# Hybrid encoder layer on one core: half-loads and a split norm at the start, joined head pairs, and another schedule for the dot products of the first expert stage

## The reference, cut to what matters

```python
h = rms_norm(x, norm1_g); z = h @ w_in            # pool (512) | q (8x64) | k, v (2x64 each)
mix = concat([pool_mixer(zp), gqa_attention(zq, zk, zv)])
x = x + mix @ w_out
xn = rms_norm(x, norm2_g)
q = (xn @ wq).reshape(.., 8, 2, 128); s = einsum(q, subkeys)
sv, si = top_k(s, 16); comb = sv[0] + sv[1]; cv, ci = top_k(comb, 16)
e = i1 * 128 + i2                                   # 16384 experts, 16 for each head and token
g = softmax(cv); a = gelu(einsum(xn, u[e])) * g
out = x + einsum(a, v[e])
```

## Time and profile before

| | |
|---|---|
| device time, median of 3 runs | 1999.72 us (1999.72 to 2002.63) |
| the profiled execution's own time | 1996.21 us |
| its span, first to last instruction | 1994.4 us |
| granted TensorE clock, mean | 0.995 |
| PE busy | 1950.4 us, 98% of the span |
| DVE, ACT, POOL busy | 1640.2, 980.4, 789.3 us |

### The profile page before, as it was taken

The page is one execution under the profiler, slowest core; times in us unless marked ns, Lnnn a source line. Parts: engine busy times, 40 slices in busy tenths (PEclk is TensorE's granted clock), DMA queues, the critical chain, the costliest instruction groups (busy, mean ns, idle before and its releaser), DMA issues.

```text
span 1994.4 us, 28888 instructions
## 1 busy us (share of the span) xinstructions
PE 1950.4 (98%) x10186; PEld 1663.6 (83%) x10186; DVE 1640.2 (82%) x3141; ACT 980.4 (49%) x2048; POOL 789.3 (40%) x588
## 2 busy tenths in 40 slices
PE   7999999999999999999999999799999999999999
PEld 7977998997888888888888888688888888888887
DVE  3866436779999999999987777699998899988997
ACT  5265333333778787777787873222223222223221
POOL 0324110001334333333355555555554555545552
PEclk9999999999999999999999999999999999999999
DMA  6110312125799989988999999899999999999996
GB/s 264 42 35 1 137 53 106 67 98 178 257 319 311 324 299 317 323 283 303 310 359 373 389 380 415 315 388 400 392 405 399 406 395 403 399 390 406 385 404 226
DMA packets 203078, 581.27 MB, mean 291 GB/s; under 512 B 19904, under 2 KB 57152, under 8 KB 200640
## 3 DMA queue, kind: packets, MB, share of 16 engines
q0 software_dynamic: 73728, 268.47, 36.7%
q1 hardware_dynamic: 77616, 243.97, 32.2%
q10 hardware_dynamic: 51600, 67.12, 9.3%
HBM read 505.03 MB, written 74.45 MB: 291 GB/s over the span
## 4 chain that ended last, share of the span: by engine, by line
PE 66%; DVE 4%; DMA 2%; ACT 2%; issue 1%; ACTq 0%; POOL 0%; SPq 0%; DVEq 0%
PE ps L332 20%; PE ps L333 20%; PE ps L334 20%; PE ps L1471 5%; DMA g_dram<-arena_a 1%; DMA arena_a<-in_uT 1%; ACT arena_a L679 1%; DMA ring_b<-in_u_rows,expert_ids 0%; ACT arena_a L683 0%; DVE w_lo L1059 0%; DVE ring_b L1149 0%; ACT arena_b L725 0%; DVE ring_a L1149 0%; DVE y_final L1245 0%; DVE ring_c L1149 0%
## 5 line engine op out<-in xcount | busy, mean ns | idle before, releaser
L332 PE MATMUL ps<-v_hi_slots,w_lo 128*128 128x512 f32 x1024 | 399.1, 390 | 6.2 <-DVE w_lo L1187 6.2
L334 PE MATMUL ps<-v_hi_slots,w_lo 128*128 128x512 f32 x1024 | 399.0, 390 | 0.0
L332 PE MATMUL ps<-feat_hi,w_hi 128*128 128x512 f32 (+1 forms) x936 | 360.0, 385 | 2.0 <-DVE feat_lo L969 2.0
L333 PE MATMUL ps<-feat_lo,w_hi 128*128 128x512 f32 (+1 forms) x936 | 351.2, 375 | 0.0
L334 PE MATMUL ps<-feat_hi,w_lo 128*128 128x512 f32 (+1 forms) x936 | 351.0, 375 | 0.0
L706 ACT ACTIVATE w_lo<-arena_a 128x512 fp32r<-128x512 f32 x128 | 80.9, 632 | 501.7 <-PE ps L334 471.3
L812 POOL DMA_INDIRECT ring_a<-in_u_rows,expert_ids x86 | 114.6, 1333 | 330.9 <-DVE ring_a L1149 169.6
L332 PEld LDWEIGHTS ps<-v_hi_slots,w_lo 128*128 128x128 f32 x1024 | 192.7, 188 | 47.0 <-issue 3.6
L334 PEld LDWEIGHTS ps<-v_hi_slots,w_lo 128*128 128x128 f32 x1024 | 192.7, 188 | 40.0
L334 PEld LDWEIGHTS ps<-feat_hi,w_lo 128*128 128x128 f32 x936 | 176.2, 188 | 31.9
L332 PEld LDWEIGHTS ps<-feat_hi,w_hi 128*128 128x128 f32 x936 | 176.6, 189 | 30.8 <-DVE feat_lo L969 2.2
(11 more groups left out here) (215 smaller groups left out, 4472.7 us busy)
## 6 DMA issues: line engine op xcount, KB each, us to landing
arena_a<-in_v SPq DMA_DIRECT2D x128, 512.0 KB, 9.4
w_raw<-in_uT SPq DMA_DIRECT2D x85, 512.0 KB, 6.6
g_dram<-arena_a ACTq DMA_DIRECT2D x64, 512.0 KB, 9.0
gel_dram<-arena_b ACTq DMA_DIRECT2D x120, 256.0 KB, 5.1
w_raw<-gel_dram SPq DMA_DIRECT2D x120, 256.0 KB, 7.8
arena_a<-in_uT SPq DMA_DIRECT2D x43, 512.0 KB, 6.6
w_raw<-in_w_all SPq DMA_DIRECT2D x17, 1024.0 KB, 5.7
arena_b<-g_dram SPq DMA_DIRECT2D x32, 512.0 KB, 10.9
```

The lines of the kernel that those rows point to most:

```text
L332: nc.tensor.matmul(out, lh, rh, start=first, stop=False)
L333: nc.tensor.matmul(out, lh, rl, start=False, stop=False)
L334: return nc.tensor.matmul(out, ll, rh, start=False, stop=last)
```

## The change

- The first weight block is loaded and split in two halves; xT slice 0 and the small vectors are issued by ACT instead of SP; SP issues the first half, xT slice 1, the second half, then the rest as before.
- PE does nine matmuls on zeroed memory before its first wait for weights; ACT's squares wait for them, since they write the same PSUM area.
- ACT squares x tiles 0 to 2, DVE squares tiles 3 to 5 ahead of `w_split_lo(1)`.
- PE takes `windows(0)` before `flip_qk(0)`; ACT takes `pooled_out(0)` before `flip_out(0)`.
- The scores and the first row maximum of the next head pair are issued within the pair before; DVE's loop over pairs is unrolled.
- The product with w_out takes its k slices in the order 4 to 7, 0 to 3, and waits for the last pair's low parts only ahead of k = 3.
- First expert stage: no dot products up to slab 16, then 2.25 a slab to the end (before: 5/3 a slab from slab 3, 13/5 from slab 81; 249 in all in both). Gate groups spread over 105 slabs for 107, top-k parts over 80 for 82, parameters of tile 0 flipped in slab 5 for 4. With the gate groups `v_first` goes from 113 to 111; SP's wait for the gate stores stays at step 120.
- Second stage: items start one step later, `a_split(1)` is made within the first stage, gate chunk 1 is loaded in steps 0 to 3 instead of ahead of them, `gelu_hid(0)` moves from step 2 to 4.

```diff
 def group_slab(g):
-    return 8 + g * 107 // NG_DEN
+    return 8 + g * 105 // NG_DEN
 def topk_slab(q):
-    return q * 82 // PARTS
+    return q * 80 // PARTS
 def dots_by(e):
-    return 5 * max(min(e - 3, 78), 0) // 3 + 13 * max(e - 81, 0) // 5
+    return 9 * max(e - 16, 0) // 4
 def items_by(e):
-    return min(ITEMS, dots_by(NK - 1) + (ITEMS - dots_by(NK - 1)) * (e + 1) // 126)
+    return min(ITEMS, dots_by(NK - 1) + (ITEMS - dots_by(NK - 1)) * max(e - 1, 0) // 124)
...
-        flip_slab = {t: softmax_step[t] + 3 if t else 4 for t in range(DT)}
+        flip_slab = {t: softmax_step[t] + 3 if t else 5 for t in range(DT)}
...
 @block.sync
-            sp.dma_start(vecs[:, :], io["vecs"]).then_inc(vec_in, 16)
-            load_w(0, 0)
-            for k in range(KD):
+            sp.dma_start(Wr[:, 0, 0:4, :], io["w_all"][0, :, 0:4, :]).then_inc(w_half, 16)
+            load_xt(1)
+            sp.dma_start(Wr[:, 0, 4:8, :], io["w_all"][0, :, 4:8, :]).then_inc(w_in[0], 16)
+            for k in range(2, KD):
                 load_xt(k)
...
-                if e == v_first + 7:
+                if e == v_first + 9:
                     sp.wait_ge(g_out[1], 16 * 4 * (NBLK // 2))
...
-            for piece in range(4):
-                load_gates(1, piece)
...
-                if e >= CH and e % CH < 4 and e // CH + 1 < NK // CH:
+                if e % CH < 4 and e // CH + 1 < NK // CH:
                     load_gates(e // CH + 1, e % CH)
...
 @block.scalar
-            w_split_hi(0)
+            act.dma_start(xst[:, 0, :], io["xT"][:, 0, :]).then_inc(xt_in[0], 16)
+            act.dma_start(vecs[:, :], io["vecs"]).then_inc(vec_in, 16)
+            act.wait_ge(w_half, 16)
+            nc.scalar.activation(Wh[:, 0, 0:4, :], Wr[:, 0, 0:4, :], ACT.Copy).then_inc(w_half_hi, 1)
...
             w_split_hi(1)
-            for t in range(TT):
+            act.wait_ge(warm, 1)
+            for t in range(3):
...
+            pooled_out(0)
             flip_out(0)
-            pooled_out(0)
...
                 if e == 126:
                     a_split_hi(0)
+                    a_split_hi(1)
...
-                if e == 2:
+                if e == 4:
                     gelu_hid(0)
...
 @block.vector
+            for t in range(3, TT):
+                dve.wait_ge(x_in[t], 16)
+                if t > 3:
+                    dve.wait_ge(sq1_dve, t - 3)
+                nc.vector.scalar_tensor_tensor(B_[:, 1536:2560], y[:, t, :], 1.0, y[:, t, :], ALU.mult, ALU.mult,
+                                               accum_out=ss1[:, t:t + 1]).then_inc(sq1_dve, 1)
             w_split_lo(1)
-            dve.wait_ge(sq1, TT)
+            dve.wait_ge(sq1, 3)
+            dve.wait_ge(sq1_dve, 3)
...
             def pair(j, first=False):
-                row_max(j, 0)
+                if first:
+                    row_max(j, 0)
                 for u in range(NU):
                     if u + 1 < NU:
                         row_max(j, u + 1)
+                    elif j < 3:
+                        row_max(j + 1, 0)
...
                 while n < dots_by(e):
-                    if n == dots_by(NK - 3) + 1:
-                        a_split_lo(0)
+                    if dots_by(NK - 3) < n <= dots_by(NK - 3) + 2:
+                        a_split_lo(n - dots_by(NK - 3) - 1)
                     dot(n)
...
+                if n == items_by(e) and e < 4:
+                    v_split_lo(e + 3)
+                    weigh(e + 2)
...
 @block.tensor
-            pe.wait_ge(w_lo, 1)
+            pe.wait_ge(zero_v, 2)
+            for i in range(9):
+                last = mm(ps[:, 7, :], KV_[:, 2 * TOK:2 * TOK + P], KV_[:, 2 * TOK:2 * TOK + 512], start=True, stop=True)
+            last.then_inc(warm, 1)
+            pe.wait_ge(w_half_lo, 1)
             for k in range(KD):
+                if k == 4:
+                    pe.wait_ge(w_lo, 1)
...
             pe.wait_ge(small_in, 16 * len(smalls))
+            pe.wait_ge(z_ev, 6 + 30)
+            windows(0)
             pe.wait_ge(rope_ok, TT // 2)
             pe.wait_ge(rope_dve, TT // 2)
             flip_qk(0)
-            pe.wait_ge(z_ev, 6 + 30)
-            windows(0)
...
                 for u in range(NU):
                     if u + 3 < NU:
                         scores(j, u + 3)
+                    elif j < 3:
+                        scores(j + 1, u + 3 - NU)
...
-            pe.wait_ge(o_lo, 2 + 8)
+            pe.wait_ge(o_lo, 2 + 6)
...
-                    for k in range(KD):
+                    for k in (4, 5, 6, 7, 0, 1, 2, 3):
+                        if k == 3:
+                            pe.wait_ge(o_lo, 2 + 8)
```

More of the change, by code:

```diff
@@ L238, in build @@
         yf = view(yf_, 0, DT, D)
-        small_in = sem("small_in")
+        small_in, warm = sem("small_in"), sem("warm")
+        sq1_dve = sem("sq1_dve")
+        w_half, w_half_hi, w_half_lo = sem("w_half"), sem("w_half_hi"), sem("w_half_lo")
         xt_in = [sem(f"xt_in{i}") for i in range(KD)]
@@ L486, in w_split_hi @@
                 nc.scalar.activation(Wh[:, n % 2, :, :], Wr[:, n % 2, :, :], ACT.Copy).then_inc(w_hi, 1)
-            w_split_hi(0)
+            act.dma_start(xst[:, 0, :], io["xT"][:, 0, :]).then_inc(xt_in[0], 16)
+            act.dma_start(vecs[:, :], io["vecs"]).then_inc(vec_in, 16)
+            act.wait_ge(w_half, 16)
+            nc.scalar.activation(Wh[:, 0, 0:4, :], Wr[:, 0, 0:4, :], ACT.Copy).then_inc(w_half_hi, 1)
             act.wait_ge(vec_in, 16)
             for k in range(KD):
+                if k == 2:
+                    act.wait_ge(w_in[0], 16)
+                    nc.scalar.activation(Wh[:, 0, 4:8, :], Wr[:, 0, 4:8, :], ACT.Copy).then_inc(w_hi, 1)
                 act.wait_ge(xt_in[k], 16)
@@ L754, in _ @@
                     act.wait_ge(a_mm, e)
-                if e + 1 < NK:
+                if 1 <= e < NK - 1:
                     a_split_hi(e + 1)
@@ L847, in newton @@
                 return tt(r, r, tmp[1], ALU.mult)
-            w_split_lo(0)
+            dve.wait_ge(w_half_hi, 1)
+            tt(Wl[:, 0, 0:4, :], Wr[:, 0, 0:4, :], Wh[:, 0, 0:4, :].bitcast(F32), ALU.subtract).then_inc(w_half_lo, 1)
             for k in range(KD):
+                if k == 2:
+                    dve.wait_ge(w_hi, 1)
+                    tt(Wl[:, 0, 4:8, :], Wr[:, 0, 4:8, :], Wh[:, 0, 4:8, :].bitcast(F32), ALU.subtract
+                       ).then_inc(w_lo, 1)
                 dve.wait_ge(ft_hi, k + 1)
@@ L955, in _ @@
             pair(0, True)
-            with dve.Fori(1, 4) as j:
+            for j in range(1, 4):
                 pair(j)
@@ L1359, in pair @@
             def pair(j, first=False):
[L1360 to L1363, removed]
                 if first:
+                    for u in range(3):
+                        if u == 2:
+                            pe.wait_ge(mix_lo, 6)
+                        scores(j, u)
                     windows(3)
@@ L1413, in _ @@
                             Wh[:, ds((c + 1) % 2, 1), k, :].squeeze(1), Wl[:, ds((c + 1) % 2, 1), k, :].squeeze(1),
-                            k == 0, k == KD - 1)
+                            k == 4, k == 3)
                     last.then_inc(y_mm, 1)
```

## The result

The changed kernel takes 2011.01 us (median; 2007.2 to 2012.39), the kernel before 1999.72 (1999.45 to 2005.95): a ratio of 1.0045, with a 95% interval of 1.0027 to 1.0062. It is slower, by 11.3 us from median to median and 8.9 from mean to mean (2001.49 to 2010.43), for 7.8 forecast; the interval is 5.4 to 12.4 us and holds the forecast.

A forecast was written before the change was run, and what follows sets the result against it. PE bounds the kernel, busy 98% of the span, with DVE nearly a bound in the first expert stage. Gains of 27.2 us and losses of 35 make 7.8 slower: 1999.72 to 2007.5 us, range 1995 to 2021 for 8 in 10.

The forecast's parts named there:

- slabs 17 to 80: First expert stage: DVE's list exceeds what PE offers by 34.9 us; 34 lost in all, ends 20 and 42.
- 5.8 of reserve: First expert stage: slack from the end of one slab to the table two slabs on hides 5.8 us of DVE's shortfall.
- The 5 us at the softmax of step 80: End of the long stretch: ACT waits for DVE, 5.8 us later, then loads two tables; 5 us more lost.
- What it said of this stage in the traces: Slabs 17 to 80: 450 to 455 us, DVE over 97% busy, PE waits in most of slabs 30 to 82, DVE's gone.
- Joined pairs: Attention, three seams between head pairs: idle time and half clock behind each go, 7.3 us gained, ends 4 and 8.5.
- The turn: Turn to the second expert stage: gate stores earlier, fewer gathered rows a slab; 16.2 us gained, ends 8 and 16.2.
- Rival B: Turn to second stage: queues stay full, PE again idles for slab 126, 16.2 us not gained, 2023.7 us; chance 0.10.
- The start: Blocks 0 and 1 of z: block 0 begins earlier, block 1 waits for the norm; 1 us lost, 0.4 gained to 2 lost.
- Slab 5 and slab 12: Early first stage: softmax wait and one-hots wait go, about 0.2 us stays; 1.0 us gained, ends 0.5 and 3.5.
- A (the overrun hides): First expert stage: DVE keeps up after all, the 34 us loss falls away, 1973.5 us; chance 0.10.
- C (the pairs don't join): Attention: ACT's loop over pairs stays a loop, so 7.3 us less gain, 2014.8 us; chance 0.06.

The follow-up runs named there:

- e1: Changed kernel with the old pace of dot products (5/3 a slab from slab 3, 13/5 from slab 81): 1984.27 us, ratio to before 0.9922.
- e2: Changed kernel with each dot product over 512 of its 1024 columns, gathers unchanged (leaves out half of each sum): 1975.7 us.
- e12: Changed kernel with 2 dot products a slab from slab 16 for 2.25, the rest left to the second stage: 2015.56 us.
- e7: Changed kernel with DVE's one-hots ahead of the low-part split in every step: 2011.62 us.
- e9: Kernel before with the joined head pairs alone, DVE's loop unrolled: 1994.28 us, ratio 0.9966.
- e4: Kernel before with gate groups over 105 slabs, top-k parts over 80, SP's wait for gate stores kept at step 120: 1996.11 us, ratio 0.9978.
- e3: Kernel before with the new pace of dot products alone (2.25 a slab from slab 16): 2018.89 us, ratio 1.0099.
- e6: Changed kernel with old dot-product pace, norm's mean and root before the split, gate groups over 103 slabs, parts over 79, SP's wait at step 120: 1990.92 us.
- e11: Changed kernel with old dot-product pace to slab 81, then 9/4 a slab, and w_split_lo(1) ahead of DVE's squares: 1987.03 us, ratio to before 0.992.
- e5: Changed kernel with the second weight block's low part made after the norm's mean and root instead of before them: 2010.31 us.
- e10: Changed kernel with the old dot-product pace and w_split_lo(1) ahead of DVE's three squares: 1981.75 us, ratio to before 0.9899.
- e8: Changed kernel without the nine matmuls on zeroed memory and ACT's wait for them: 2012.81 us.

## Why the prediction was right, and which of its terms were not

**The sum and its main cause held.** The step "slabs 17 to 80" foresaw 29 us from DVE's list (457.8 us, against 422.9 that PE offers and 5.8 of reserve); 28.5 were measured. e1 and e2 show the cause from two sides (undo the rule, or halve DVE's time at the same gathers: 422 us both times), e12 its slope, and e7 shows that it isn't an order within the step.

Of the 28.5, 19.0 are idle time of PE and 9.5 stand in the busy column (429.13 for 419.68). e1 runs the same 2168 instructions of PE without the long list, and subtracting the spacings one by one tells what the 9.5 are. The one table more that the change has in the stretch is 0.4 (e1 has 420.10). Two stretches of 3.4 us at half clock, from 597.0 and 743.8 us, are 3.0. After has 23 waits there and e1 2; at each of the 21, 0.16 us is lost because the matmul ahead, 0.39 us long, isn't overlapped by one that starts 0.23 us later, 3.4 in all. Behind 19 of the waits, and once elsewhere, the second instruction of a table starts 0.21 us after the first and not 0.11, 2.1 in all; 0.5 is spread over the rest. As long as DVE's list sets the pace, such losses of PE only take the place of idle time, and the total stays the list's.

The 5 us at the softmax of step 80 were 7.8: one wait of 4.9 us for ACT (L700), and 6.8 us at half clock behind it, of which the prediction had none. What it said of this stage in the traces held but for two points: PE waits for one-hots in 20 of the 53 slabs from 30 to 82, not in most of them, and DVE's waits for ACT's splits didn't go but fell only from 9.3 to 5.7 us.

The whole, 7.8, is the difference of 35 lost and 27.2 gained. Between the two profiled executions (14.8 for 7.8) the single terms of the table err by 3 us at most and by 7.0 in all, all but three of them towards slower.

**Joined pairs: 7.3 was too much, 4.6 measured** (after and e9 alike). The failed step is "3 × (0.72 + 1.7)": the 0.72 us of idle time per seam was counted as a cost. e4's seam at full clock shows that it is none, and the half clock measured 1.5 us a seam, not 1.7.

**The turn: 16.2 foreseen, 18.0 measured, by another mixture of causes.** The prediction named the earlier stores and the lower rate together and took the stores for nearly all of it. Counted from gelu 85, since gelu 120 itself is late in e1 and e4, the earlier stores alone give 6.7 us (e4), the rate alone 9.2 (e3), all of the change but the rate 9.4 (e1), and all of it 17.8. Still earlier stores gave nothing (e6). What remains of the wait in e1 hangs on the landing of the last gate store in full queues (DMA share 1.03 from 1200 to 1250 us), as the 5.8 us between e1 and e11 show; about 1 us more is DVE's chain from the landed slab to that low part (19.0 us in e1, 17.9 in e11). Rival B, that the turn stays, didn't come.

**The start: right in size (+1.18 for +1), by luck.** The prediction had block 1 begin at 30.50 as before and lose 1 us to half clock behind 4 us of idle time. Block 1 begins at 31.59, 1.09 later, behind 2.48 us of idle time, and no half clock follows it (z has full clock from 13.33 us on). Its sum of 30.5 took 25.0 us for the start of the last square, which is 26.08 in after; with that it gives 31.6. That it also gave before's 30.50 was chance: in before the first eviction had started at 28.96, and block 1 has no idle time ahead of it, so it was held by PE's own block 0 and not by the norm. The list of what follows the last square named the right instructions, but e5 shows that block 1 needs the split for itself, not only through the mean; the split would have had to go ahead of the squares (e10). PE began block 0 only 1.7 us earlier (10.24 for 11.92), where I had estimated 4: its first wait ends with a low part of xT (L866), not with the half of the weights. Before's execution was also a lucky one: e3, e9 and e4 have its start unchanged, their clock first rises at 15.38, 16.38 and 17.17 us for 14.72, and z ends 0.4, 0.7 and 1.2 us later. Against e4 the change loses nothing at the start.

**Slab 5 and slab 12: 1.0 foreseen, 0.1 by gelu 16.** The wait of 2.7 us for the softmax became one of 3.1 for the low part of slab 5 (L1083), which DVE makes right behind that softmax. I had named this successor and sized it at 0.2. Six kernels here have the lists of after up to slab 16; in two of them (e7, e8) 6.8 us at half clock follow this wait, and gelu 0 to 16 takes 2.5 and 2.6 us longer than before. The other half of the term held: e3, with the later start of the dot products alone, gains 1.1 there. It is the largest of the small errors in reasoning: a wait that is removed doesn't help where the next need is served by the same engine directly after it.

**Not foreseen: 2.5 us between w_out and gelu 0.** The clock falls twice there in after. Two windows, of after:

```profile
286.40:289.81 3.41, 3.41 (x18) 3.41 (x17) 3.34 (x8) 2.70 (x4) 2.78 (x2) 0.50 0.56 228
300.05:303.46 3.41, 3.13 (x7) 2.48 (x8) 2.52 (x2) 1.10 (x2) 0.00 (x0) 0.50 1.02 406
```

The waits in front (longest 1.98 us, for L993) are the same in every kernel here. Before, e3 and e10 had full clock there, e4, e6, e7, e9 and e11 one fall, after, e1, e2, e5, e8 and e12 two; it costs 1.6 or 2.5 us. Kernels with the same instructions in this place fall none, one or two times, so the code there doesn't settle it. But two falls occur only in kernels with the whole change or nearly all of it (6 of 10), never in the four built on before; whether the change makes them likelier stays open.

**A (the overrun hides) and C (the pairs don't join)** are refuted, A by PE's 20.9 us of idle time in the stretch, C by pairs of 22.69 us for 24.15.

## What to carry to other kernels

Ask of each stage, not of the whole kernel, how much an engine that works from a list has left: list time against the time that the bound engine offers, plus the reserve of a step or two. Beyond that, each piece of work costs nearly its full length, here 1.0 us for a dot product of 1.14, while the share of the whole span says nothing (82% in both kernels). Work that is moved out has to be priced where it arrives (0.7 to 0.8 us in a stage whose queues are full), and a part of a change that is wrong can hide the gain of the others, so measure the parts apart: all but one line of this change is worth 15 us, and with one split moved the kernel takes 1981.75.

## What the runs showed of the hardware that was not expected

- At one seam an idle time of PE of 0.72 us cost nothing by itself (e4), while the half clock that can follow it cost 1.5 us for 3.4 us of it; whether it follows differs between executions with the same waits. One seam is no rule: in the first expert stage the idle stretches aren't made good, and behind most waits PE loses some 0.26 us more (0.16 of overlap, 0.10 at the second instruction).
- In e4's execution PE had 23.9 us at half clock from 194.66 us on while it was busy (the second row shown under e4, clock 0.57 in the mean): some 9 us of that execution, in a place where no other execution here has it. Differences of single executions below that size need a stretch by stage, or many times.
- With the queues at about 410 GB/s a store of 512 KB took 28.43 us (e1) or 26.46, and it held what waited for it. It was the last of four issued some 6 us apart; in e1 they took 17.4, 22.5, 26.6 and 28.4 us. At the turn e6 issued it two slabs earlier still and gained nothing, since other transfers of 13.6 to 25.3 us took its place.
